# Issuing the modulation pieces of a two-layer encoder trunk from ScalarE instead of SyncE

## What is computed

```python
c_act = jax.nn.silu(c)
for l in range(DEPTH):
    ada = (c_act @ w_ada[l] + b_ada[l]).reshape(B, N_ADA, D_MODEL)          # N_ADA = 9
    u = _modulate(_rmsnorm(x, norm_g[l, 0]), ada[:, 0], ada[:, 1])
    x = x + 0.5 * ada[:, 2][:, None, :] * _swiglu(u, w_ff1_up[l], w_ff1_down[l])
    u = _modulate(_rmsnorm(x, norm_g[l, 1]), ada[:, 3], ada[:, 4])
    x = x + ada[:, 5][:, None, :] * _token_mixing(u, w_in[l], ...)
    u = _modulate(_rmsnorm(x, norm_g[l, 2]), ada[:, 6], ada[:, 7])
    x = x + 0.5 * ada[:, 8][:, None, :] * _swiglu(u, w_ff2_up[l], w_ff2_down[l])
```

## Time and profile before

| | |
|---|---|
| median of three runs | 2031.03 us (2030.36 to 2033.58) |
| profiled execution: its own time | 2033.83 us |
| profiled execution: span from the first to the last instruction | 2032.0 us |
| mean granted TensorE clock | 0.995 |
| TensorE busy | 2004.0 us (99%) |
| VectorE busy | 1019.5 us (50%) |
| GpSimd busy | 671.4 us (33%) |
| ScalarE busy | 557.0 us (27%) |
| moved by DMA | 264.72 MB, mean 130 GB/s |
| issues of pieces, SP | 128 of 512 KB |
| issues of upward loads, SP | 176 of 512 KB |

### The profile page before, as it was taken

One profiled execution on the slowest core, in us unless ns is written; L12 is line 12 of the kernel. 1 busy time (PEld: TensorE's weight loads), 2 busy tenths in 40 slices (PEclk: granted clock), 3 DMA queues, 4 the chain that ended last, 5 costly groups with the idle time before them and its releaser, 6 DMA issues.

```text
span 2032.0 us, 24087 instructions
## 1 busy us (share of the span) xinstructions
PE 2004.0 (99%) x9895; PEld 1677.6 (83%) x9895; DVE 1019.5 (50%) x1500; ACT 557.0 (27%) x810; POOL 671.4 (33%) x269
## 2 busy tenths in 40 slices
PE   6899999999999999999999999999999999999999
PEld 5788888888788888888898888889788898888888
DVE  4585356584656765311267743657654766311121
ACT  3222122234522322122232222223253233221221
POOL 0355445401000245444434463452100005543451
PEclk8999999999999999999999999999999999999999
DMA  9656376522224376333426644663221335323331
GB/s 274 182 166 210 93 205 198 119 73 79 77 73 152 96 208 191 100 104 95 133 63 194 209 146 141 187 196 71 92 76 58 119 115 156 116 81 93 95 114 62
DMA packets 354038, 264.72 MB, mean 130 GB/s; under 512 B 49850, under 2 KB 335882, under 8 KB 353930
## 3 DMA queue, kind: packets, MB, share of 16 engines
q1 hardware_dynamic: 352256, 262.70, 43.8%
q10 hardware_dynamic: 1674, 0.50, 0.1%
HBM read 261.07 MB, written 2.10 MB: 130 GB/s over the span
## 4 chain that ended last, share of the span: by engine, by line
PE 94%; DVE 2%; DMA 2%; ACT 1%; issue 0%; ACTq 0%; POOL 0%; SPq 0%; DVEq 0%
PE bank L1377 27%; PE bank L1379 27%; PE bank L1378 27%; PE bank L1449 1%; PE bank L1453 1%; PE bank L1450 1%; PE bank L1404 1%; PE bank L1405 1%; PE bank L1406 1%; DMA stage<-in_w_ff_up 1%; PE ps L1557 1%; PE ps L1538 1%; DMA stage<-in_w_ff_down 0%; PE bank L1665 0%; PE ps L1545 0%
## 5 line engine op out<-in xcount | busy, mean ns | idle before, releaser
L610 POOL TENSOR_TENSOR w_lo<-stage,w_hi 128x1024 fp32r<-128x1024 f32 (+1 forms) x236 | 649.3, 2771 | 1185.2 <-ACT w_hi L657 1137.3
L1377 PE MATMUL bank<-u_hi,w_hi 128*128 128x512 f32 x1768 | 698.4, 395 | 3.9 <-POOL w_lo L610 3.6
L1379 PE MATMUL bank<-u_hi,w_lo 128*128 128x512 f32 x1768 | 690.3, 390 | 0.0
L1378 PE MATMUL bank<-u_lo,w_hi 128*128 128x512 f32 x1768 | 690.2, 390 | 0.0
L657 ACT ACTIVATE w_hi<-stage 128x1024 fp32r<-128x1024 f32 (+2 forms) x335 | 348.8, 1074 | 595.5 <-DMA stage<-in_w_ff_up 339.8
L1377 PEld LDWEIGHTS bank<-u_hi,w_hi 128*128 128x128 f32 x1768 | 332.8, 188 | 77.3 <-issue 5.1
L1378 PEld LDWEIGHTS bank<-u_lo,w_hi 128*128 128x128 f32 x1768 | 333.0, 188 | 70.0 <-issue 2.4
L1379 PEld LDWEIGHTS bank<-u_hi,w_lo 128*128 128x128 f32 x1768 | 332.8, 188 | 70.0
L1377 PE MATMUL bank<-h_hi,w_hi 128*128 128x512 f32 x744 | 289.9, 390 | 0.6 <-POOL w_lo L610 0.6
L1046 DVE TENSOR_TENSOR prod<-silu,bank 128x512 f32<-128x512 f32 x88 | 60.5, 688 | 457.1 <-PE bank L1379 428.0
L1379 PE MATMUL bank<-h_hi,w_lo 128*128 128x512 f32 x744 | 289.8, 390 | 0.0
(11 more groups left out here) (174 smaller groups left out, 1482.0 us busy)
## 6 DMA issues: line engine op xcount, KB each, us to landing
stage<-in_w_ff_up SPq DMA_DIRECT2D x176, 512.0 KB
ada_stage<-in_w_ada SPq DMA_DIRECT2D x128, 512.0 KB, 5.1
stage<-in_w_ff_down SPq DMA_DIRECT2D x32, 1408.0 KB
stage<-in_w_in SPq DMA_DIRECT2D x16, 1024.0 KB
ada_block<-in_w_ada SPq DMA_DIRECT2D x8, 1024.0 KB, 11.9
stage<-in_w_out SPq DMA_DIRECT2D x8, 1024.0 KB
stage<-in_w_in SPq DMA_DIRECT2D x40, 128.0 KB
stage<-in_w_in SPq DMA_DIRECT2D x10, 512.0 KB
```

Source lines behind the costliest of these rows:

```text
L610: nc.gpsimd.tensor_tensor(stage_tile(w_lo, kind, n), t, hi_tile(n, depth(kind, n)), ALU.subtract).then_inc(lo_ready, 1)
L1377: mm(bank[n % BANKS][:, :], hi[:, k, :], rhs_hi(k), start=(k == 0), stop=False)
L1378: mm(bank[n % BANKS][:, :], hi[:, k, :], rhs_lo(k), start=False, stop=False)
L1379: last = mm(bank[n % BANKS][:, :], lo[:, k, :], rhs_hi(k), start=False, stop=(k == k_n - 1))
```

## The change

SP's loop over the loads of a half no longer issues pieces. The function `ada_piece` moves to ScalarE's program, with the same waits, and is called in its loop over tiles: at tile 1 pieces 0, 1 and 2, at every tile n from 4 on piece n-1, after the tile's rounding and silu. The pieces so go on ScalarE's DMA queue. Piece n-1 waits there for the use of piece n-4, which VectorE does at its tile n-1. In the first half of the kernel the issues of pieces 0 to 2 stand ahead of those of the positions and sinks.

```diff
@@ SP: def ff_half(l, i, half, up, down)
-                sent = 0
                 for n in range(FF_LOADS):
...
-                    while (sent < ff_pieces(l, i, half) and 2 * n >= (sent + ADA_SLOTS if sent >= ADA_SLOTS else 0)
-                           and (n >= STAGE_SLOTS - 1 or l + i + half)):
-                        ada_piece(l, i, half, sent)
-                        sent += 1
-                assert sent == ff_pieces(l, i, half)
@@ SP
-            def ada_piece(l, i, half, a):
-
-                g, k = divmod(a, KT)
-                src = w_ada.rearrange("l (k p) n -> l k p n", p=P)
-                free = pieces_before(l, i, half) + a + 1 - ADA_SLOTS
-                if free > 0:
-                    sp.wait_ge(ada_used, free)
-                else:
-                    sp.wait_ge(block_done, BLOCKS)
-                v = 2 + half * FF_GROUPS + g if i == 0 else (N_ADA - 1 + g) % N_ADA
-                sp.dma_start(ada_stage[a % ADA_SLOTS][:, :], src[l + (i > 0 and g > 0), k, :, v * D:(v + 1) * D]
-                             ).then_inc(ada_in[a % ADA_SLOTS], 16)
@@ ScalarE
+            def ada_piece(l, i, half, a):
+
+                g, k = divmod(a, KT)
+                src = w_ada.rearrange("l (k p) n -> l k p n", p=P)
+                free = pieces_before(l, i, half) + a + 1 - ADA_SLOTS
+                if free > 0:
+                    act.wait_ge(ada_used, free)
+                else:
+                    act.wait_ge(block_done, BLOCKS)
+                v = 2 + half * FF_GROUPS + g if i == 0 else (N_ADA - 1 + g) % N_ADA
+                act.dma_start(ada_stage[a % ADA_SLOTS][:, :], src[l + (i > 0 and g > 0), k, :, v * D:(v + 1) * D]
+                             ).then_inc(ada_in[a % ADA_SLOTS], 16)
@@ ScalarE: def ff_half(l, i, half)
                         nc.scalar.activation(silu[:, j % 2, :], bank[n % BANKS][:, :], ACT.Silu
                                              ).then_inc(silu_ready, 1)
+                    if n:
+                        for a in range(ADA_SLOTS) if n == 1 else range(max(n - 1, ADA_SLOTS), n):
+                            if a < ff_pieces(l, i, half):
+                                ada_piece(l, i, half, a)
                     if l + i + half == 0 and n == 2:
                         positions_load()
```

## The result

The change makes the kernel slower: the median of ten runs is 2038.0 us (2036.9 to 2039.2), against 2031.5 for the kernel before in the same rounds; ratio 1.0032, 95% interval 1.0022 to 1.0042. The forecast was 2024.7 us, 6.3 us faster, with a range up to 2031.5; the measured median is 6.5 us slower and outside it.

The account below looks back on a forecast made before the run. Bound by matmuls: TensorE busy 2004.0 of 2032.0 us. Regained 3.72 + 2.93 + 0.76, less 1.1 at tile 6, gives 6.3 us faster: 2024.7 from the median of 2031.03; range 2022.7 to 2031.5.

Parts of the forecast that it names:

- The price of the low clock: Behind the gap at tile 8, 14 matmul steps at the lower clock: 2.93 us expected to be regained.
- (a): Tile 8, first half: its wait for weights goes because their load is issued earlier, 3.72 us regained.
- (c): Tile 22, first half: its wait for weights goes, 0.76 us regained.
- (d): Tile 5, first half: three issues on ScalarE take 1.40 us before its rounding; 0.9 us to spare, no cost.
- (f): The other 125 pieces: 59 us more on ScalarE, three us of slack at the tightest spot, cost zero.
- (e): Tile 6, first half: pieces 0 to 2 share the way with its load, landing at 70.5; 1.1 us more idle.
- a third of the way up, because of that room: Choice of 70.5 for the landing of tiles 6 and 7, from a range of 70 to 71 between the bounds.
- upper bound: Load of tiles 6 and 7 with all three pieces ahead, less 0.7 us for the positions: 3.1 us later.
- R2: Tile 6: its load is held by the sinks, landing at 77.4; 3.5 us slower, 2034.5 us; chance 0.08.
- R1: Tile 6: slower load, wait over 2 us and low clock again; 2029.6 or 2028.5 us; chance 0.23.
- the wait that the change takes away: SP issues the load of tiles 8 and 9 only at 69.27, behind piece 3, though its slot was free at about 62.3.
- a second cause: Load of tiles 8 and 9 took 14.41 us; from 69 to 76 us only 693 packets moved, the sinks' 4-byte elements.

Follow-up runs that it names:

- later halves alone: Kernel before in its first half, the changed kernel in all later halves, so 104 pieces go through ScalarE: 2030.7 us, ratio 1.0000.
- SP's order turned round: Kernel before, with SP issuing the load of tiles 8 and 9 ahead of piece 3 in the first half, all pieces still on SP: 2027.7 us, ratio 0.9982.
- sinks early: Changed kernel, with the sinks' four issues moved from tile 2 to between the third and fourth block on ScalarE: 2030.1 us, ratio 0.9995.
- in 128 packets: Changed kernel, with the sinks loaded by one issue of 128 packets of 64 bytes, not 1024 of 4 bytes: 2030.7 us, ratio 0.9996.
- both repairs: Changed kernel, with pieces 0 to 2 of the first half back on SP and the sinks issued between the third and fourth block: 2027.4 us, ratio 0.9982.

## Why the prediction was wrong

**The bound and the places were right.** TensorE sets the time; the two gaps for weights were the only ones in reach, and both went. Nothing else that shows in the time moved, by the run with the later halves alone. The price of the low clock was right in size, though 1.6 and 3.1 us (busy time times the missing share of the clock) stand behind the same gap.

**(a) held.** The load of tiles 8 and 9, issued early, crawls beside the sinks and comes in time: 18.7 us after the first silu with SP's order turned round, where the sum's landing at 80 (held until 77, then 3 us) was 18.4. **(c) and (d) held** by their numbers: tile 22 has no wait, and the three issues took 1.32 us where 1.40 was taken. For (c) that is not proof: in the changed kernel `sin_t` took 0.48 us, as in the two runs that have no wait there with SP's order of before. **(f) held in its sum** (zero), with less room than written: after the mixing of layer 0 the load of tiles 6 and 7 is now rounded 11.5 us after the first silu of its half (705.85 and 694.37), and was at 5.8 before; I had allowed for 3.8 later and it is 5.7, with no sinks about. About 1.5 us of slack are left (ready at 709.4, wanted at 710.9), not three.

**The step that failed is (e)**, the price of putting three pieces beside the load of tiles 6 and 7. I took a landing at 70.5, 8.9 us after the first silu, and 1.2 us of idle; they were 19.0 and 11.1. Two errors are in it. The smaller: "a third of the way up, because of that room". With the sinks out of the way the pieces delay the load by 3.1 us (sinks early) and 3.7 (in 128 packets), the whole upper bound or more; the room was none. That gives an idle of 3.0 and 3.6 us at tile 6 where 1.2 was taken, and with it the low clock. The larger: the upper bound ended with the pieces' bytes. It left out what the load meets when it is pushed back, the sinks, though the earlier trace rows stood in the same argument for the next load. The delay is no sum of two prices: with neither the load lands at 7.6 to 8.2, with the sinks alone at 7.7 to 8.0, with the pieces alone at 10.9 to 11.5, with both at 19.0. The sinks cost this load nothing by themselves and 7.4 to 8.1 us once the pieces are ahead.

**R2 named this mechanism** and got a chance of 0.08. It was priced with the pieces of the middle case and the sinks' 7 us, a landing 15.8 us after the silu, and 3.5 us slower; the true terms are 3.1 and 8.1, and the loss 6.5. Its argument against, "the sinks come a us later than before, and then this load passed ahead of them", looked at the sinks alone: they came one us later, but the load three. R1 (1.4 to 2.5 us faster) is what the runs with the sinks away and the pieces ahead show, 0.5 to 1.4 us under the kernel before; their intervals (0.9986 to 1.0004, 0.9987 to 1.0005) include no difference at all.

**The cause of the gap before was named in the wrong order.** The prediction called SP's wait behind piece 3 "the wait that the change takes away" and the sinks "a second cause". Either is enough to close the gap at tile 8: turning SP's order round does it with the sinks in place, and thinning the sinks does it with SP's wait in place, and the second is the faster by the medians (2024.2 and 2027.7), though the two intervals still touch (0.9950 to 0.9975 and 0.9973 to 0.9990). The change took the one away and made the other decide.

The Trainium skill's rule used against the change (DMA: Bandwidth & Descriptors, "Issuing engines are not separate DMA queues") holds in its main part: no bandwidth was gained, and the transfers interleave, as the packets of 72 to 74 us show. The prediction's "the trace agrees" pointed at the wrong row for it: from 69 to 76 us none of SP's packets moved, which is no interleaving. The rule's other half, that the issue's time is usually small beside the transfer itself, does not fit the run with the pieces behind the sinks: there three issues took 8.27 us, and the three pieces would take 3.8 by the prediction's estimate. The rule on turns packet by packet (same page, "Queues, rings and completion order") would have two queues advance with equal counts, if the packets that the profile counts are those of the rule. For the load and the sinks the trace shows 212 and 215; for the load and the pieces it does not agree, 408 against 120 from 62 to 64 us and 263 against 206 from 66 to 68. The pieces got more of the bytes, as R1 argued, but with fewer packets and not with equal turns. The rule would not by itself say why only some 100 packets of each pass in a us, nor why before no packet of SP's queue passed at all for 7 us; what paces them is not shown by any run here.

## What to carry to other kernels

When a transfer is moved, write down what the transfers beside it will meet when they are late, not only how late they become: here a load without slack, pushed by three us, came into a stretch that held it for eight more. Look for broadcasts of single elements among the transfers: here 1024 packets of 4 bytes stopped or slowed the weight loads for some nine us, and loading whole rows and picking the columns on VectorE took that away. Before a wait is engineered out of a queue, double and remove the traffic that shares the way: here this one issue was worth some 7 to 8 us, and the change of queue cost 6.5.

## What the runs showed beyond that

- The sinks pass at about 100 to 113 packets a us, whether alone (693 in 7 us, 902 in 8 us) or beside a load (788 in 8 us), and take 4 to 5% of the DMA engines' time: the busy share of the DMA engines does not show this bound.
- An issue is not always cheap for its engine: 0.33 to 0.58 us with the way free; 4.03 and 4.45 us on SP beside the pieces and behind a load, with the sinks in 128 packets; 2.5 to 7.6 us with the 4-byte sinks under way, on SP (two in 12.50 us; one of 7.61 in the changed kernel, from 71.84) and on ScalarE (three in 8.27 us). So the sinks are not the only thing that makes an issue slow.
- Runs of one kernel spread by up to 5 us (2025.8 to 2030.7 us for SP's order alone), and here is a part of it. In some executions a load of the second mixing's last matrix takes longer (6.96 to 7.24 us) and opens a gap of 1.8 to 2.0 us at its first tile, in others (5.27 to 5.41) it opens none or one of 0.2. The chain of waits of the kernel before, and then of the run with SP's order turned round:

```profile
1610.07 5.27 DMA stage<-in_w_out
```
```profile
1603.03 6.96 DMA stage<-in_w_out
```

In the second the clock fell behind the gap, for another 1.7 us; in the run with both repairs, after a gap of 2.0 at the same place, it did not. What makes that load slower in some executions was not tried.
